# Gated recurrence: the output gate's second column chunk computed between the levels of the first eight slots

## What is computed

```python
z = x @ w_in_l
(c_h, c_b, c_c, g_q, g_f, g_i, g_g, ...) = jnp.split(z, SPLIT_POINTS, axis=-1)
f = lb_l + (1 - lb_l) * sigmoid(g_f);  kk = (1 - lb_l) * (1 - sigmoid(g_f))
b = cumsum(log f) within a chunk
inter = (q * exp(b)) @ S
att   = sum over k of q[t] * exp(b[t] - b[s]) * kk[s], for s <= t
intra = att @ v
S_new = exp(b_last) * S + (kk * exp(b_last - b)).T @ v
o_hg  = (inter + intra) * rsqrt(mean square + eps) * hg_norm
y_hg  = o_hg * sigmoid(g_g)
```

## Time and profile before

| | |
|---|---|
| time, median of 3 runs | 4292.5 us (4289.4 to 4299.4) |
| the profiled execution | 4295.7 us, its span 4293.5 us |
| TensorE busy | 3882.1 us, 90% |
| VectorE / ScalarE / GpSimd busy | 2055.1 us (48%) / 977.0 us (23%) / 1180.3 us (27%) |
| mean granted TensorE clock | 0.919 of full speed |
| L889, feature matmuls | 1152 records, 379.5 us |
| L949, products of the slots | 1088 records, 127.6 us |

### The profile page before, as it was taken

The page is one execution under the profiler, slowest core; times in us unless marked ns, Lnnn a source line. Parts: engine busy times, 40 slices in busy tenths (PEclk is TensorE's granted clock), DMA queues, the critical chain, the costliest instruction groups (busy, mean ns, idle before and its releaser), DMA issues. The chain is left out here.

```text
span 4293.5 us, 50474 instructions
## 1 busy us (share of the span) xinstructions
PE 3882.1 (90%) x19162; PEld 2689.9 (63%) x19162; DVE 2055.1 (48%) x4141; ACT 977.0 (23%) x1922; POOL 1180.3 (27%) x1047
## 2 busy tenths in 40 slices
PE   6899987889997999999879998878899979999996
PEld 4344564444566998889643445644445668888985
DVE  5799555432144333333567994554221343333335
ACT  2201224421122122111231012344111222111222
POOL 3014672223022212112330156632130231212213
PEclk8899957999997999999979999589999889999998
DMA  3111003460211111111020110044501111111111
GB/s 139 41 43 47 6 1 104 146 231 0 79 35 64 39 57 41 39 39 39 10 95 28 39 43 6 2 158 148 174 23 56 40 67 51 39 39 39 47 41 42
DMA packets 143022, 254.97 MB, mean 59 GB/s; under 512 B 24577, under 2 KB 76162, under 8 KB 142594
## 3 DMA queue, kind: packets, MB, share of 16 engines
q1 hardware_dynamic: 130562, 215.00, 14.6%
q0 software_dynamic: 12288, 37.76, 2.6%
HBM read 231.31 MB, written 21.42 MB: 59 GB/s over the span
## 5 line engine op out<-in xcount | busy, mean ns | idle before, releaser
L2357 PE MATMUL ps<-ffn_parts 128*128 128x512 f32 (+1 forms) x3456 | 801.8, 391 | 7.4 <-DVE arena L2487 7.4
L2347 PE MATMUL ps<-ffn_parts 128*128 128x384 f32 (+1 forms) x4608 | 779.7, 330 | 25.9 <-POOL ffn_parts L2432 25.9
L2347 PEld LDWEIGHTS ps<-ffn_parts 128*128 128x128 f32 x4608 | 775.3, 189 | 31.2 <-POOL ffn_parts L2432 26.9
L2357 PEld LDWEIGHTS ps<-ffn_parts 128*128 128x128 f32 (+1 forms) x3456 | 623.4, 182 | 174.7 <-DVE arena L2487 24.2
L2487 DVE TENSOR_TENSOR arena<-arena,ps 128x1024 f32<-128x1024 f32 (+1 forms) x288 | 351.2, 1219 | 342.5 <-PE ps L2357 338.4
L889 PE MATMUL ps<-arena,arena_rest 128*128 128x512 f32 (+1 forms) x1152 | 379.5, 492 | 3.7 <-PEq L445 2.7
L2437 POOL TENSOR_TENSOR ffn_parts<-arena,ffn_parts 128x1024 fp32r<-128x1024 f32 x64 | 154.2, 2409 | 611.3 <-ACT ffn_parts L2391 611.3
L899 PE MATMUL ps<-arena_rest,arena 128*128 128x512 f32 (+3 forms) x864 | 318.7, 526 | 2.3 <-ACT arena_rest L1072 2.3
L889 PEld LDWEIGHTS ps<-arena,arena_rest 128*128 128x128 f32 x1152 | 191.8, 193 | 193.5 <-issue 192.1
L322 DVE TENSOR_SCALAR_CACHE_REDUCE arena_rest<-arena_rest,small 128x384 bf16<-128x384 f32 (+4 forms) x330 | 278.8, 875 | 2.1
L1941 PE MATMUL ps<-arena_rest,arena 128*128 128x512 f32 (+1 forms) x576 | 254.4, 601 | 22.0 <-DMA arena_rest<-in_w_out 22.0
(11 more groups left out here) (291 smaller groups left out, 5036.2 us busy)
## 6 DMA issues: line engine op xcount, KB each, us to landing
arena_rest<-in_kv SPq DMA_DIRECT2D x128, 256.0 KB, 9.4
arena<-in_w_down SPq DMA_DIRECT2D x32, 1024.0 KB, 7.6
arena_rest<-in_w_in SPq DMA_DIRECT2D x10, 2048.0 KB, 8.1
ffn_raw<-in_w_up SPq DMA_DIRECT2D x16, 1024.0 KB, 5.8
arena<-in_w_up SPq DMA_DIRECT2D x16, 1024.0 KB, 5.9
out_y_prompt<-arena SPq DMA_DIRECT2D x3, 4096.0 KB, 15.9
arena<-out_y_prompt SPq DMA_DIRECT2D x2, 4096.0 KB, 24.7
arena_rest<-in_mem_kT SPq DMA_DIRECT2D x16, 512.0 KB, 7.2
```

What stands on the lines that cost most here:

```text
L2347: ins = pe.matmul(bank(3 * c + b, y - x), w[:, k, :], h[:, k, x:y], start=(k == 0 and h is HH and w is WH), stop=(k == KC - 1 and w is WL))
L2357: ins = pe.matmul(bank(b0 + a)[0:R, :], u[:, c, tcol(t)], d[:, c, 512 * a:512 * a + 512], start=(c == 0 and u is UH and d is DH), stop=(c ...
```

## The change

The output gate's first chunk (feature 10) is still computed ahead of the recurrence. Its second chunk is no longer a feature: its 24 matmuls (8 contraction chunks times three) are issued one by one, each behind the products of a tile in slots 0 to 7, into PSUM columns 2560 to 3647 (`gate`). Since `XT` and the gate's weights are read until slot 7 ends, other things move:

- the gate's weights get a place of their own, `WG`, at W 6016; they are loaded at the same point as before;
- TensorE waits for eleven copies before slot 0;
- the start exponential goes straight into `QT`, and its columns at the chunk ends are computed separately into two small tables `EP` and `ES`; the query product is formed in place;
- ScalarE's order is `level(1)`, end-gate exponential, copy of feature 10, `EP`, `ES`, start exponential, `level(2)`; at the end of iteration 7 it waits for the gate's last matmul and copies the second chunk; the sigmoid and its table loads stand in iteration 8, behind `level(8)`;
- GpSimd's clearing (now a wait for the gate's last matmul) is at the head of iteration 8, and the gate's product in iteration 9;
- VectorE's convolution copy is in iteration 9, behind a wait for the gate's last matmul;
- the load of the sample states no longer waits for features.

```diff
+    WG = at("W", 6016, KC, 256)
+    EP, ES = (e["stat"][:, 16 * n:16 * n + 16].rearrange("p (c n) -> p c n", c=2) for n in range(2))
...
-                    sp.dma_start(WB[n % 2][:, :, 0:w],
+                    sp.dma_start(WB[n % 2] if n < 5 else WG,
...
-            sp.wait_ge(s_fp, 12)
             sp.wait_ge(s_up, 3 * NT)
...
-            for c in range(2):
-                feat(10 + c, WB[1], c)
-
-            pe.wait_ge(s_fe, 12)
+            feat(10, WG, 0)
+            pe.wait_ge(s_fe, 11)
             pe.wait_ge(s_ue, 3 * NT)
+
+            def gate(n):
+                k, (a, b) = n // 3, ((0, 512), (512, 1024), (1024, TOK))[n % 3]
+                ins = pe.matmul(ps[:, 2560 + a:2560 + b], WG[:, k, P:2 * P], XT[:, k, a:b],
+                                start=(k == 0), stop=(k == KC - 1), skip_group_check=True)
+                if n == 3 * KC - 1:
+                    ins.then_inc(s_gp, 1)
...
+                        if g == 0:
+                            gate(3 * n + t)
...
-            feat()
             level(1)
-            feat()
             act.wait_ge(s_kd, 1)
             act.activation(KH, KH, ACT.Exp).then_inc(s_kx, 1)
-            act.wait_ge(s_fp, 12)
-            act.activation(E0, BB, ACT.Exp).then_inc(s_e0, 1)
+            feat()
+            act.activation(EP, BB[:, :, P - 1:SEQ:P], ACT.Exp)
+            act.activation(ES, BB[:, :, SEQ + DT - 1:TOK:DT], ACT.Exp)
+            act.activation(QT, BB, ACT.Exp).then_inc(s_e0, 1)
+
+            def gate():
+                act.wait_ge(s_gp, 1)
+                act.copy(GG[:, 1, :], ps[:, 2560:2560 + TOK]).then_inc(s_ge, 1)
...
                 if k == 7:
-                    act.wait_ge(s_fe, 12)
+                    gate()
+                if k == 8:
+                    act.wait_ge(s_fe, 11)
+                    act.wait_ge(s_ge, 1)
                     act.activation(GG, GG, ACT.Sigmoid).then_inc(s_sg, 1)
                     act.preload_act_table_set("natural_log_exp_and_others")
...
-            pool.wait_ge(s_fp, 12)
-            pool.wait_ge(s_up, 3 * NT)
-            pool.memset(at("W", 6016, 1536), 0.0).then_inc(s_hz, 1)
             for k in range(len(work)):
+                if k == 8:
+                    pool.wait_ge(s_gp, 1)
+                    pool.memset(at("W", 6016, 1536), 0.0).then_inc(s_hz, 1)
...
-                if k == 8:
+                if k == 9:
                     pool.wait_ge(s_sg, 2)
...
-                    ch(dve.tensor_tensor(QT, GQ, E0, ALU.mult))
+                    ch(dve.tensor_tensor(QT, GQ, QT, ALU.mult))
                     dve.engine_nop().then_inc(s_qs, 1)
-                if k == 3:
+                if k == 9:
+                    dve.wait_ge(s_gp, 1)
                     dve.wait_ge(s_cv, 1)
                     ch.mark(dve.tensor_copy(YT[:, 0:2, :], CB))
```

More of the change, by code:

```diff
@@ L759, in mixer_block @@
     s_D = [sem(f"hg_diff{c}") for c in range(2)]
-    s_kx, s_e0, s_gg, s_nv, s_nl = (sem(n) for n in (
-        "hg_end_exp", "hg_start_exp", "hg_gate_out", "hg_mean_sq", "hg_mean_sq_log"))
+    s_kx, s_e0, s_gp, s_ge, s_nv, s_nl = (sem(n) for n in (
+        "hg_end_exp", "hg_start_exp", "out_gate_done", "out_gate_copied", "hg_mean_sq", "hg_mean_sq_log"))
     s_hz, s_ap, s_ad, s_kp, s_ke, s_pp, s_sv, s_op, s_oe = (sem(n) for n in (
@@ L771, in mixer_block @@
     VB = at("S", 2 * TOK, 4, DB, HD)
-    E0 = at("A", 4 * TOK, 2, TOK)
+    WG = at("W", 6016, KC, 256)
+    EP, ES = (e["stat"][:, 16 * n:16 * n + 16].rearrange("p (c n) -> p c n", c=2) for n in range(2))
     GL = [at("C", 0, 2, 384), at("S", 4 * TOK, 2, 384), at("C", 768, 2, 384)]
@@ L1365, in state @@
                         ins = dve.scalar_tensor_tensor(st(t + 1)[:, c, :], st(t)[:, c, :],
-                                                       E0[:, c, t * P + P - 1:t * P + P],
+                                                       EP[:, c, t:t + 1],
                                                        bank(7)[:, c * HD:(c + 1) * HD], ALU.mult, ALU.add)
@@ L1374, in state @@
                     x = S0[:, :, c, :]
-                    last = E0[:, c, SEQ:TOK].rearrange("p (b s) -> p b s", b=DB)[:, :, DT - 1:DT]
-                    ch(dve.tensor_tensor(x, x, last.broadcast_to([P, DB, HD]), ALU.mult))
+                    ch(dve.tensor_tensor(x, x, ES[:, c, :].unsqueeze(2).broadcast_to([P, DB, HD]), ALU.mult))
                 dve.wait_ge(s_pp, NT)
```

## The result

The changed kernel takes 4312.5 us (median of 7 runs, 4305.6 to 4322.9) against 4292.5 before (7 runs too, 4289.4 to 4299.4). The ratio is 1.0045, 95% interval 1.0032 to 1.0057: slower by some 19 us, where 22 us faster was forecast. The profiled execution has a span of 4313.3 us against 4293.5, 19.8 more.

The account below looks back on a forecast made before the run. TensorE was taken to bound the start of slot 0, GpSimd slots 0 to 7, TensorE at half clock later. Per layer 15.0 + 0.95 - 4.7 = 11.2 us; 4292.5 - 22.4 = 4270.1 us, range 4258 to 4289.

Parts of the forecast that it names:

- The start: Ahead of slot 0: with the second chunk gone, the first product comes at 514.35 instead of 529.37, gain 15.0 us a layer.
- the term that I took as 0.5 between 0 and 2.4: At the start: delay in us of VectorE's end difference by GpSimd's first multiplications, now beside it.
- part 2: Slots 0 to 7 with three gate matmuls each: GpSimd's pace stays, level 7 ready 29.55 us after the start.
- I take full clock: Slots 0 to 7: gate work fills the pause that lowered the clock, leaving about 2 us idle before slots 3 and 4.
- The size of a slot: TensorE in slots 0 to 7: 3.5 to 3.9 us at full clock, against GpSimd's 3.91; 6.7 at half.
- rivals B and C: Clock falls in slots 3 and 4: B, it comes back, about 4281, 19%; C, it stays down to slot 7, 15%.
- rival C: Slots 3 to 7 at half clock, five at 2.8 us: 4298 to 4314, one layer only 4287; 15%, a third one-layer.
- The hand-over: Slots 7 to 10: slot 11 begins 24.0 us after level 7 is ready instead of 19.3, a loss of 4.7 a layer.
- part 3: Slots 7 to 10: chain of gate copy, level 8, clearing, sigmoid with table loads, level 9, gate's product, level 10; 24.0 us.
- 0.95 was in my sum: Slot 3: the convolution copy leaves it, and with it 0.95 us of GpSimd's stretch a layer.
- After slot 11: Slots 11 to 23: they run at half clock, bound by TensorE, as before.

Follow-up runs that it names:

- e1_one_chunk: The changed kernel with seven of the gate's eight contraction chunks left out, the three matmuls of slot 7 staying; 4282.4 us.
- e3_filler: The changed kernel with eight unused 512-column matmuls added a layer, in the pauses of slots 2 to 5; 4291.8 us.
- e6_grouped: The changed kernel with each slot's three gate matmuls in a row behind its first tile, not one behind each tile; 4297.5 us.
- e7_level8_first: The changed kernel with ScalarE's level 8 exponential ahead of its wait for the gate in iteration 7; 4313.5 us.
- e5_late_product: e4 with only GpSimd's gate product put back to slot 9, behind level 9's multiplications; 4276.2 us, once more 4274.2 us.
- e2_ahead: The changed kernel with all 24 gate matmuls ahead of slot 0, right behind feature 10, other engines' order kept; 4285.5 us.
- e10_start_order: The changed kernel with ScalarE's copy of feature 10 and level 2's exponential ahead of the end-gate exponential; 4312.5 us.
- e8_filler_all: e5_late_product with two unused 128-column matmuls added to every tile from slot 4 to slot 23; 4342.5 us.
- e4: The changed kernel with the gate in slots 0 to 3, in rows of three; its copy, sigmoid, product and the convolution copy moved; 4282.3 us.
- e9: e5_late_product with the gate's chunks laid 1, 1, 2, 2, 1, 1 over six slots, gate and convolution copies in slot 6; 4267.9 us.

## Why the prediction was wrong

**The start held.** Forecast: first product at 514.35, gain 15.0. Measured: 515.55, and 14.5 from the projection's start. The missing part is the term that I took as 0.5 between 0 and 2.4. VectorE's end difference beside GpSimd's four multiplications:

```profile
508.41 4.02 DVE L1347 TENSOR_TENSOR arena_rest<-arena_rest 128x1024 f32<-128x1024 f32 x4
```

It took 4.02 instead of 2.82, 1.2 more, and the end-gate exponential and the copy behind it came that much later. The Trainium skill's rule on the two engines' shared access (SBUF — State Buffer, "Who interferes with whom") agrees in kind; of its 2.4 a half was paid. This cost about 0.5 us a layer of the sum. What I had not priced is that the later copy makes TensorE's pause ahead of slot 0 2.19 us instead of 1.16: the clock dips behind it (below).

**The slots failed, in three terms of part 2.**
- The clock. "I take full clock" was the step. I had foreseen pauses of about 2 us before slots 3 and 4; there were three shorter ones, 1.07 and 0.72 us ahead of the third tile of slots 2 and 3, and 0.69 ahead of slot 4. I had the row that speaks on them, 0.80 of 4 us busy, and reasoned that more work than that would do. The clock fell behind 534 to 537 with TensorE busy 1.77 of 3 us. `e1_one_chunk` shows that the loss is in the gate work of the slots, and `e3_filler` that the clock and not the amount makes it: more work, full clock, 9.9 us less.
- The size of a slot. Forecast 3.5 to 3.9 us at full clock and 6.7 at half; measured 4.26 (`e3_filler`) and 7.78. I had priced the gate's matmuls from the unbroken projection and a tile's products from unbroken slots. Alternated, a 512-column matmul costs 1.05 us at full clock and 2.0 at half, and a tile's products 1.05 at half, not 0.94: 2 x 2.0 + 0.62 for the narrow matmul + 3 x 1.05 = 7.8. So a slot at half clock lost 3.5 on one at full clock, not 2.8.
- What brings the clock back (weighed in rivals B and C). I gave the stay at half to slot 7 15% against 19% for a return, since half of a slot is 512-column work like the projection's. At half clock TensorE was busy 30.82 of 31 us with that work, and the clock did not return. `e6_grouped` shows that the same matmuls in rows of three do bring it back. The same single matmuls had ended the dip in slot 0. What counts is more than the busy share and the kind of matmul; what it is stays open. By the cut this term makes the sign: `e6_grouped`, where the clock falls too but comes back, has slots of 39.1 instead of 52.7 and a sum 5.5 under before.

By the forecast slots 0 to 7 were to take 29.55 + 3.8 = 33.4 us. They took 52.7: 19.3 of the 20.4 us a layer by which the forecast (11.2 gained) misses the cut (9.2 lost). The start and the hand-over are 0.5 each. Of the 19.3, 14.1 are the clock in slots 4 to 7 (four slots at 3.5), and 1.6 its dip in slot 0; most of the remaining 3.6 is by an estimate the dearer slot at full clock (4.26 instead of 3.91, eight times 0.35). That is rival C by its mechanism, in both layers, over four slots and not its five. The time lies in its span of 4298 to 4314, near the upper end: that five slots at 2.8 and four at 3.5 come to the same 14 is luck, and the dip and the dearer slots come on top. The rule of the Trainium skill that spoke against the change (TensorE: Matmul & The Clock Gate, "HAM oscillation — how this bites in real kernels") was borne out on the fall, by pauses of 0.69 to 1.07 us. I had cited it, and weighed it too low.

**The hand-over held.** Forecast 24.0 from level 7's being ready, of which 3.8 is slot 7: 20.2 from its end. Measured 20.7. The chain is the one in part 3, now in the rows above: gate copy at 568.38, level 8's exponential, table load, level 9's at 574.83, multiplication, product at 578.14, slot 11 at 588.99. GpSimd waits 8.99 us for level 8 and not 4.5, since slot 7 came late. `e7_level8_first` takes level 8 out of that chain and gains 0.7 only, so the sigmoid with its tables and the product are what remain. `e5_late_product`, with the gate done by slot 3 and its sigmoid back in slot 7, took 15.8 with the product still in slot 9.

**What I had not seen: part of the moves has a gain of its own.** `e2_ahead` keeps the gate's second chunk ahead and is 3.9 us a layer faster. Not all of it was in the change. The 1.2 at the start come from that run's own order, whose gate matmuls cover the copy; the changed kernel still waits for it. Of the 2.7 in the slots, 0.95 was in my sum, for the convolution copy. How much the changed kernel had is told by slots 0 to 6 where they hold no gate: 30.6 us before, 27.9 in `e2_ahead`, 29.2 in `e1_one_chunk`, which has the changed kernel's order. So at least 1.4 was there, 0.4 more than forecast, and hidden by the slots that TensorE bound.

**After slot 11** nothing changed, as forecast: half clock, 94.8 us in both.

## What to carry to other kernels

Work that is put into the pauses of a latency-bound loop must leave none of them long enough for TensorE's clock to fall: look up in the trace beside which pauses it fell, and lay more of the work there (here 1, 1, 2, 2, 1, 1 chunks instead of one in each of eight slots). Put large matmuls in rows, not singly between small ones: here that cost less at full clock, and the clock came back. And ask what was queued behind the result: its copy, its table loads and its product want slots of their own on the other engines, not the first one that comes (hand-over 20.7 against 15.1).

## What the runs showed of the hardware

- TensorE can be busy without a gap and stay at 1.2 GHz: 30.82 of 31 us in the changed kernel, 34.00 of 34 in `e10_start_order`, 144.29 of 148 with small matmuls in `e8_filler_all`. The same work in rows of three 512-, 512- and 64-column matmuls came back to 2.4 GHz within 3.5 us (`e6_grouped`). But it did so too with single 512-column matmuls between 128-column products (slot 0 of the changed kernel), and once, at 2796 of `e8_filler_all`, with small matmuls alone.
- A pause of 2.19 us behind the unbroken projection was followed by a fall of the clock in slot 0 in every run that had it (changed, e1, e3, e6, e7), in both layers; one of 1.16 us in none (before, e4, e5, e8, e9, e10).
- At full clock the alternation itself costs some 0.3 us a slot (4.26 against 3.96).
- Filler can pay: eight large matmuls more a layer took 9.9 us off the slots, since they kept the clock.
- The same 1503 matmuls of the attention stage take 172.8 us or 176.9, at a mean clock of 0.95 or 0.92, by how the kernel ahead of them is shifted. What in the shift decides was not tried.
- Open: why single matmuls between the 64-column products of slots 4 to 7 didn't bring the clock back, and those in slot 0 did; no run here varied the pattern further. That the size of a group matters is shown for one and three only, and where a group stands in time may matter as well.
